# Modulation weights loaded from SyncE's queue instead of GpSimd's, their slots given back one step earlier

## What is computed

```
def adaln_modulation(cond, w_ada, b_ada):
    return jnp.split(jax.nn.silu(cond) @ w_ada + b_ada, N_MOD, axis=-1)
...
    mods_lat = [m[:, None, :] for m in adaln_modulation(c, ada_w[layer], ada_b[layer])]
    mods_ctx = adaln_modulation(c_ctx, ada_w[layer], ada_b[layer])
    x = ffn_sublayer(x, *mods_lat[0:3], ffn_w_gu[layer, 0], ffn_w_down[layer, 0], ln_g[layer, 0], ln_b[layer, 0])
```

## Time and profile before

| | |
|---|---|
| median of 3 runs | 2601.47 us (2600.58 to 2601.55) |
| the profiled execution | 2601.47 us, its span 2599.7 us (1.8 us lie around it) |
| busy share of the span | TensorE 96%, VectorE 66%, ScalarE 47%, GpSimd 31% |
| mean granted TensorE clock | 0.987 |
| DMA | 359 MB, mean 138 GB/s; SyncE's queue 283 MB, GpSimd's 73 MB |

### The profile page before, as it was taken

How to read it: one execution, slowest core, us unless ns; L and a number is a source line. 1 busy time by engine, 2 the same in 40 slices (tenths; PEclk the granted TensorE clock), 3 DMA queues, 4 the chain that set the end, 5 groups by cost and what they waited for, 6 DMA issues and landing times.

```text
span 2599.7 us, 42985 instructions
## 1 busy us (share of the span) xinstructions
PE 2496.8 (96%) x16456; PEld 2171.9 (84%) x16456; DVE 1727.7 (66%) x3440; ACT 1216.2 (47%) x2307; POOL 808.0 (31%) x878
## 2 busy tenths in 40 slices
PE   8999999997889999999999998999999999999998
PEld 6788887876778888888888887889998889998998
DVE  4787587998777786455864446666663576746766
ACT  4333325661254433325333325755555578555684
POOL 0332232013214332223221223032135543655435
PEclk9999999998989999999999999999999999999999
DMA  6554452220002554443553432236544444544444
GB/s 255 198 199 167 159 178 72 73 82 3 3 9 81 183 207 145 138 138 106 190 178 110 166 126 90 89 128 235 190 155 141 144 150 143 165 151 144 152 137 145
DMA packets 101404, 359.05 MB, mean 138 GB/s; under 512 B 13136, under 2 KB 15312, under 8 KB 100816
## 3 DMA queue, kind: packets, MB, share of 16 engines
q1 hardware_dynamic: 78800, 282.89, 31.8%
q0 software_dynamic: 22400, 73.42, 8.7%
HBM read 355.20 MB, written 1.05 MB: 137 GB/s over the span
## 4 chain that ended last, share of the span: by engine, by line
PE 76%; DVE 12%; ACT 6%; issue 3%; POOL 2%; DMA 1%; DVEq 0%; POOLq 0%; ACTq 0%; SPq 0%
PE ps L1958 21%; PE ps L1961 21%; PE ps L1959 21%; DVE spl L2553 2%; DVE work L2577 1%; DVE big L2577 1%; ACT spl L2307 1%; PE ps L2022 1%; DVE big L2771 1%; PE ps L2215 1%; PE ps L1983 1%; PE ps L1985 1%; PE ps L1984 1%; POOL spl L3038 1%; POOL bigr L3043 1%
## 5 line engine op out<-in xcount | busy, mean ns | idle before, releaser
L1958 PE MATMUL ps<-bigr,spl 128*128 128x256 f32 (+1 forms) x3846 | 1306.4, 340 | 19.6 <-DVE spl L2553 11.5
L1961 PE MATMUL ps<-bigr,spl 128*128 128x256 f32 (+1 forms) x3846 | 1288.7, 335 | 3.5 <-POOL bigr L3043 3.2
L1959 PE MATMUL ps<-bigr,spl 128*128 128x256 f32 (+1 forms) x3846 | 1285.9, 334 | 0.0
L2553 DVE TENSOR_TENSOR spl<-ring,spl 128x512 fp32r<-128x512 f32 x838 | 660.2, 795 | 559.4 <-ACT spl L2307 555.7
L2307 ACT ACTIVATE spl<-ring 128x512 fp32r<-128x512 f32 x1024 | 630.2, 627 | 633.8 <-PE ps L1961 593.0
L1958 PEld LDWEIGHTS ps<-bigr,spl 128*128 128x128 f32 x3846 | 731.4, 190 | 111.1 <-issue 13.7
L1961 PEld LDWEIGHTS ps<-bigr,spl 128*128 128x128 f32 x3846 | 730.8, 190 | 84.1 <-POOL bigr L3043 10.5
L1959 PEld LDWEIGHTS ps<-bigr,spl 128*128 128x128 f32 x3846 | 731.6, 190 | 73.9 <-issue 1.7
L3043 POOL TENSOR_TENSOR bigr<-work,bigr 128x512 fp32r<-128x512 f32 (+1 forms) x196 | 203.5, 1041 | 747.0 <-ACT bigr L2311 746.8
L3038 POOL TENSOR_TENSOR spl<-ring,spl 128x512 fp32r<-128x512 f32 x186 | 252.1, 1356 | 276.2 <-ACT spl L2307 275.8
L2311 ACT ACTIVATE bigr<-work 128x512 fp32r<-128x512 f32 (+1 forms) x224 | 117.0, 525 | 337.2 <-DVE work L2637 239.3
(11 more groups left out here) (314 smaller groups left out, 2421.4 us busy)
## 6 DMA issues: line engine op xcount, KB each, us to landing
ring<-w_stream SPq DMA_DIRECT2D x512, 512.0 KB, 3.4
big<-w_stream POOLq DMA_DIRECT2D x280, 256.0 KB, 4.3
big<-w_stream SPq DMA_DIRECT2D x16, 512.0 KB, 10.2
X<-x_t SPq DMA_DIRECT2D x2, 1024.0 KB, 15.4
cst<-consts SPq DMA_DIRECT2D x1, 1537.5 KB, 8.6
X<-mem_t SPq DMA_DIRECT2D x1, 1024.0 KB, 5.6
out_t<-X SPq DMA_DIRECT2D x8, 128.0 KB, 2.1
prm<-params SPq DMA_DIRECT2D x1, 252.5 KB, 2.7
```

The source lines that it names most:

```text
L1958: pe.matmul(out, hi, x[0], start=k == 0, stop=False)
L1959: pe.matmul(out, lo, x[0], start=False, stop=False)
L1961: finish(pe.matmul(out, hi, x[1], start=False, stop=k == nk - 1), tile, key if k == nk - 1 else None)
L2553: dve.tensor_tensor(lo_half(h), raw_half(h), hi_half(h), SUB).then_inc(*sig("lo", h, by="lo_dve"))
```

## The change

SyncE issues the loads of the modulation weights and of the condition's rows, at the places of the list where GpSimd did. A slot is given back as soon as the vector step that reads it is written, so the load written ahead of vector step j waits for the end of step j-1 instead of j-2. Nothing that is computed changes.

```diff
@@ ada_vec
-                coming, past, read = [], [], []
+                coming, past = [], []
...
                         yield "ada_vec", p, l, g, j, conds, slot, a, crow, past[-2:-1]
                         past.append(("ada_k", l, g, j))
-                        read.append(si)
-                        if len(read) > 1:
-                            slots.give(read.pop(0), past[-2])
+                        slots.give(si, ("ada_k", l, g, j))
                         yield CUT
-                for si, key in zip(read, past[-1:]):
-                    slots.give(si, key)
@@ sync_program
+            def ada_load(j, slot, free, si):
+                a = j % 2 * HC
+                w.all(free, done)
+                sp.dma_start(slot, W[n_main + j // 2][:, a:a + HC]).then_inc(*sig("ada_in", j, by=f"ada_in{si}", n=16))
+
+            def cond_load(p, r, row, free):
+                w.all(free, done)
+                sp.dma_start(row, W[n_main + r // 2][:, r % 2 * HC:r % 2 * HC + HC]).then_inc(*sig("cond_in", p, r, by="cond_in", n=16))
...
-            run({f.__name__: f for f in (start, load, load_memory, store)})
+            run({f.__name__: f for f in (start, load, ada_load, cond_load, load_memory, store)})
@@ gpsimd_program
-            def ada_load(j, slot, free, si):
-                a = j % 2 * HC
-                w.all(free, done)
-                pool.dma_start(slot, W[n_main + j // 2][:, a:a + HC]).then_inc(*sig("ada_in", j, by=f"ada_in{si}", n=16))
-
-            def cond_load(p, r, row, free):
-                w.all(free, done)
-                pool.dma_start(row, W[n_main + r // 2][:, r % 2 * HC:r % 2 * HC + HC]).then_inc(*sig("cond_in", p, r, by="cond_in", n=16))
```

More of the change, by code:

```diff
@@ L3100, in index_start @@
                 pool.tensor_copy(IDX, P("causal")).then_inc(*sig("idx_start", l))
-            run({f.__name__: f for f in (tables, ada_load, cond_load, split_lo, dual, acc_pool, pads, decay, decayed, unit, q_decay,
+            run({f.__name__: f for f in (tables, split_lo, dual, acc_pool, pads, decay, decayed, unit, q_decay,
                                          head_rest, rope, index_start)})
```

## The result

The changed kernel takes 2616.02 us (median of 4 runs, 2615.55 to 2622.34) against 2601.44 before (4 runs, 2600.58 to 2601.55): ratio 1.0061, 95% interval 1.0049 to 1.0074, 14.6 us slower. Run once more on another chip beside three experiments it gave 1.0058 (1.0045 to 1.0070). The span of the profiled execution grew from 2599.7 to 2612.5 us.

What follows compares the result with a forecast made beforehand. TensorE was busy 96%, but VectorE already set the pace in f = 0. Losses of 11.3 (f = 0) and 7.6 (f = 1) less 2.4 (f = 3) gave +16.5 on 2601.5: 2618 us, range 2597 to 2645.

Steps and rivals of the forecast that it cites:

- idle time per pair: VectorE standing still for a late ring chunk in each gate and up pair: 5.18 needed less 3.82 available, 1.36 us.
- landing: Time for a ring chunk issued behind a slot load to arrive: taken as 4.0 us, ends 3.3 and 5.3.
- f = 0: First dense stretch of the modulation stream: 14 waits cost 19.0 us, less 4.7 and 3.0, net loss 11.3.
- f = 1: Second dense stretch of the modulation stream: 14 pairs lose 0.88 us each, 12.3, less 4.7, net loss 7.6.
- v1: Vector step written after a pair's first half; the next ring load can't be issued before it ends, leaving 3.82 us.
- head start: VectorE's lead at the start of f = 0 and f = 1 from earlier first loads: worth 4.7 us in each.
- f = 3: Six first loads go out earlier and no longer meet the ring's, so TensorE's 2.4 us loss goes away.
- late streams: Modulation streams beside down, with VectorE at half load and splits up to three halves ahead: no cost.
- f = 2: Stretch with 51 vector steps for 60 places; pairs without a step make good the others' losses: no cost.
- Hidden and faster: Rival, chance 0.13: chunks land in time and only the gains stand, -6.8 us, 2594.7 us.
- Even: Rival, chance 0.2: landings of 3.2 to 3.5 or a larger head start cancel gain and loss, 2599 to 2606 us.
- Heavier: Rival, chance 0.12: landings as long as the worst in f = 0, or a second late load, 2645 to 2660 us.

Runs made afterwards that it cites:

- e6: Changed kernel with only the first loads of each stream back on GpSimd: ratio 1.0124 to the kernel before, 32 us slower.
- e7: Changed kernel with SyncE keeping each slot load's wait in place but issuing that load after the ring's next load: ratio 0.9980 to the kernel before.
- e1: Changed kernel with slots given back one vector step late, as before, SyncE still issuing all loads: ratio 0.9972 to the kernel before, 7.3 us faster.
- e3: Kernel before with only the first loads of each stream (condition rows and four slots) moved to SyncE: ratio 0.9963, 9.6 us faster.
- e5: Changed kernel with the ring's loads written one chunk earlier in the list: ratio 0.9979 to the kernel before, 5.5 us faster.
- e2: Kernel before with slots given back one step earlier, GpSimd still issuing the loads: ratio 1.0003.
- e4: e2 with SyncE also carrying out the slot loads' waits but issuing none of them: ratio 1.0036 to the kernel before, 9.4 us slower.
- e8: Changed kernel run again beside e3, e6 and e7: ratio 1.0058 to the kernel before.

## Why the prediction was right

**The idle time per pair.** Forecast 1.36 us with a landing of 4.0. Measured in the changed kernel: the landing of the 14 chunks in f = 0 is 4.00 on average, and the idle time 1.19; in f = 1 over 13 chunks 4.01 and 1.25. In 12 of the 14 pairs the idle time is 0.9 to 2.4 us and in two it is nil. In those two the doubled vector step falls between v1 and the split, and gives the chunk 1.34 us more; I had counted the wait in all 14. The landing of 4.0 was my choice between 3.5 and the medians; the forecast hangs on it (2601 us at 3.3, 2654 at 5.3), and that it was met to the hundredth is in part luck.

**f = 0.** Forecast a gain of 3.0 and a loss of 19.0 - 4.7 = 14.3, net 11.3. Measured 5.0 and 14.9, net 9.9. The gain was mis-sized: the stall of 3.0 us had a sequel in TensorE's clock (below). Within the loss two terms were off in opposite directions. The waits came to 14 x 1.19 = 16.7 us, not 19.0; the head start was worth 18.0 - 14.9 = 3.1 against e6, not 4.7 (the first slow split of the stream ends 3.6 us before TensorE needs it). That the loss was met within 0.6 us is partly luck.

**f = 1.** Forecast 7.6, measured 17.7 - 11.1 = 6.6. The head start was there: the tightest split after the start of the stream ends 4.5 us before TensorE needs it, where it ended 0.4 us ahead in the kernel before. I had put 4.7. (36 matmuls of 0.226 us are 8.1, not 8.2; with that my own sum gives 4.6.)

**f = 3 and the rest.** Forecast a gain of 2.4, measured 2.9. As forecast, the late streams and f = 2 cost nothing: the delay stands still from 264 to 400 us and from 1033 to 1570.

**Sum.** 16.5 us forecast, 12.9 in the profiled execution, 14.6 by the medians. The three terms come to 9.9 + 6.6 - 2.9 = 13.6; the other -0.7 comes from other parts of the span, of which the forecast had nothing. The 2618 us forecast are 2 us above the measured 2616.0.

**The rivals.** "Hidden and faster" needed a wait under 0.3 us per pair. It is just what e7 made (0.26), and e7 was faster. "Even" needed landings of 3.2 to 3.5 or a larger head start; they took 4.0, and the head start was no larger. "Heavier" needed landings over 5: they occur (5.15 and 5.46, once in each stretch), but not in every pair. That issuing engines matter little because they share the DMA engines (the Trainium skill, DMA: Bandwidth & Descriptors, "Issuing engines are not separate DMA queues") is true here of the transfers: e1 and e3, with all loads on SyncE and with most on GpSimd, differ by 0.1%, within their intervals. It leaves out a queue in which one load waits in front of another; there the same 280 loads cost 15 us or gain 5.5, as e5 shows.

## What to carry to other kernels

Before a load is moved to a queue that prefetches, look at what it waits for: every load written behind it inherits that wait, and a prefetch that ran well ahead is tied to the compute engine that it feeds. If the load must be there, give it an older wait (e1), or write the prefetch ahead of it (e5, e7). Moves of this kind are worth taking apart: here the loads with waits long fulfilled (e3) brought all the gain, and those with fresh waits all the cost.

## What the runs showed of the hardware

A short stall of TensorE cost more than its length. In the kernel before it stood still for 3.0 us until 75.89; then the granted clock was 0.57 on average from 76 to 80 us, and only 11 matmuls began in these 4 us. In the kernel after there is no stall, the clock is at 1.00, and 19 begin. The lower level is 1.2 GHz and the upper 2.4. Busy time by stretch of the kernel before, columns as in the earlier trace rows:

```profile
70.00:76.00 6.00, 3.00 (x14) 2.18 (x13) 0.69 (x1) 2.56 (x5) 0.91 (x2) 1.00 0.93 336
76.00:80.00 4.00, 4.00 (x11) 3.14 (x12) 2.63 (x6) 1.78 (x5) 0.00 (x0) 0.57 0.35 131
```

And of the kernel after:

```profile
70.00:76.00 6.00, 6.00 (x28) 4.99 (x27) 4.78 (x11) 2.10 (x4) 1.29 (x1) 1.00 0.12 44
76.00:80.00 4.00, 4.00 (x19) 3.30 (x19) 3.77 (x10) 0.21 (x1) 0.00 (x0) 1.00 0.74 242
```

Those 8 matmuls are 8 x 0.227 = 1.8 us, which with the 3.0 make 4.8 of the 5.0 measured. The other traces agree: from 60 to 82 us the clock was 0.92 in e2, e4 and e6, where TensorE stood still for 2.9 to 3.2 us at the same place, and 1.00 in e1, e3, e5 and e7, where it didn't. In e8 a stall of 2.0 us at 247.7 was followed by a lower clock (0.83 from 246 to 256 us). The shorter stalls of the kernel after, up to 1.5 us each, were not, from 100 to 232 us (1.00). Nor is every long stall: TensorE stands still for 2.75 us just before 35 us in the kernel before and in e3 alike, and from 34 to 39 us the clock was 0.66 in the one and 1.00 in the other.

How long a chunk of the ring took to land went with what was issued next to it. For the odd chunks of f = 0, on average: 4.8 us in the kernel before and in e3, where GpSimd issues a slot load 0.4 us ahead of the chunk; 4.3 in e1 and 4.0 in the changed kernel, where SyncE issues one 0.4 us ahead; 3.8 in e4 and 3.4 in e7, where GpSimd or SyncE issues it 0.2 and 0.4 us behind. No run shows why GpSimd's loads weigh more.
